# A two-layer hybrid decoder step on one core: where split operands are made and in which order they are queued

## The reference, cut

```python
x = LN(ALPHA * x + 0.5 * (silu(x @ w_gate) * (x @ w_up)) @ w_down)      # first feed-forward, width 2816
h = x @ w_in                      # pooling input | q | k | v | cross q | three gates of 1024
y_pool = causal pooling, four windows;  y_swa = sliding-window attention;  y_x = attention into 256 memory rows
merged = sum(sigmoid(gate_b) * (y_b @ w_br_b) for b in 3 branches)
x = LN(ALPHA * x + merged @ w_o)
x = LN(ALPHA * x + 0.5 * (silu(x @ w_gate) * (x @ w_up)) @ w_down)      # second feed-forward
```

## Time and profile before

| what | value |
|---|---|
| runs of the kernel before | 2546.69, 2549.53, 2554.24 us; median 2549.53 |
| profiled execution, device time | 2552.91 us |
| its span of instructions | 2551.1 us |
| granted clock of TensorE, mean | 0.982 |
| busy: PE, PEld, DVE, ACT, POOL | 2442.1, 2374.3, 1631.7, 1221.1, 615.6 us |
| instructions | 45264 |
| DMA | 220.63 MB, mean 86 GB/s |

### The profile page before, as it was taken

How to read it: one execution, slowest core, us unless ns; L and a number is a source line. 1 busy time by engine, 2 the same in 40 slices (tenths; PEclk the granted TensorE clock), 3 DMA queues, 4 the chain that set the end, 5 groups by cost and what they waited for, 6 DMA issues and landing times.

```text
span 2551.1 us, 45264 instructions
## 1 busy us (share of the span) xinstructions
PE 2442.1 (96%) x17684; PEld 2374.3 (93%) x17684; DVE 1631.7 (64%) x2716; ACT 1221.1 (48%) x2459; POOL 615.6 (24%) x544
## 2 busy tenths in 40 slices
PE   6999999999999999999999999989999999999997
PEld 6999999899999889999989999979999998999996
DVE  2878776435444587777687777664443447878775
ACT  4555555334422365655465556542342225655653
POOL 1333333120000123333323333321100002333332
PEclk9999999989999999999999999989999999999999
DMA  6132223222122212232213222222112222222221
GB/s 222 63 120 83 100 88 122 67 75 56 51 82 75 83 67 100 75 106 86 100 50 110 91 100 88 105 90 94 43 55 75 75 75 83 71 96 100 81 103 54
DMA packets 53523, 220.63 MB, mean 86 GB/s; under 512 B 15520, under 2 KB 18464, under 8 KB 40224
## 3 DMA queue, kind: packets, MB, share of 16 engines
q1 hardware_dynamic: 53312, 217.74, 25.1%
...
## 4 chain that ended last, share of the span: by engine, by line
PE 78%; DVE 12%; ACT 5%; DVEq 2%; issue 2%; DMA 0%; POOL 0%; ACTq 0%
PE pair L1796 12%; PE pair L1798 11%; PE pair L1797 11%; PE pair L1648 9%; PE pair L1650 9%; PE pair L1652 9%; PE S L1734 2%; DVE htl L1104 2%; PE S L1796 2%; PE S L1798 2%; PE S L1797 2%; ACT hth L660 1%; PE S L1890 1%; DVE TP L1024 1%; PE TP L1950 1%
## 5 line engine op out<-in xcount | busy, mean ns | idle before, releaser
L1796 PE MATMUL pair<-xth,hiA 128*128 128x288 f32 x1216 | 358.9, 295 | 13.9 <-ACT c L712 7.8
L1797 PE MATMUL pair<-xtl,hiA 128*128 128x288 f32 x1216 | 358.8, 295 | 0.0
L1798 PE MATMUL pair<-xth,loA 128*128 128x288 f32 x1216 | 358.4, 295 | 0.0
L612 ACT ACTIVATE hiA<-TP 128x512 fp32r<-128x512 f32 (+1 forms) x372 | 194.0, 555 | 220.0 <-DVE TP L1029 136.0
L1562 POOL TENSOR_TENSOR loB<-rawB,hiB 128x512 fp32r<-128x512 f32 (+1 forms) x128 | 159.5, 1247 | 480.2 <-ACT hiB L612 480.2
L1010 DVE TENSOR_TENSOR loA<-rawA,hiA 128x1024 fp32r<-128x1024 f32 x108 | 133.9, 1240 | 218.7 <-ACT hiA L599 218.3
L1648 PE MATMUL pair<-xh,hiA 128*128 128x288 f32 x1088 | 253.8, 310 | 18.9 <-DVE loA L1010 9.0
L1015 DVE TENSOR_TENSOR loA<-TP,hiA 128x512 fp32r<-128x512 f32 (+1 forms) x372 | 236.3, 635 | 31.7 <-ACT hiA L612 29.0
L1650 PE MATMUL pair<-xl,hiA 128*128 128x288 f32 x1088 | 243.0, 300 | 0.0
L1652 PE MATMUL pair<-xh,loA 128*128 128x288 f32 x1088 | 242.7, 300 | 0.0
L1796 PEld LDWEIGHTS pair<-xth,hiA 128*128 128x128 f32 x1216 | 228.0, 187 | 15.4 <-issue 15.3
...
## 6 DMA issues: line engine op xcount, KB each, us to landing
...
mcs<-in_mks SPq DMA_DIRECT2D x2, 2048.0 KB, 10.0
```

What stands on the lines that cost most here:

```text
L612: nc.scalar.activation(slot((hiA, hiB), prod, n), src, ACT.Copy).then_inc(f_hi, 1)
L1796: nc.tensor.matmul(bank, wt_hi, xt[0], start=start, stop=False, skip_group_check=True)
L1797: nc.tensor.matmul(bank, wt_hi, xt[1], start=False, stop=False, skip_group_check=True)
L1798: last = nc.tensor.matmul(bank, wt_lo, xt[0], start=False, stop=i == n - 1, skip_group_check=True)
```

## The change

Nothing is computed otherwise; the same products and sums are made. Blocks of the change:

1. Memory stage: the value pairs (pairs 1 and 3) get a split place of their own (`mwh`, `mwl`), so that ACT may round a pair while PE reads the one before; the copies of `x` move on ACT to behind pair 0, and on DVE to behind pair 2; the first fills of the feed-forward move to behind pair 2.
2. Feed-forward, head and first unit (u = 3): other places on ACT and DVE for the fills of unit 3, for the rounding of pair 0 and pair 1 of the hidden values, and for the copy `u2`.
3. Hidden pairs 3, 6 and 9: their first two forms are rounded in the iteration behind the four D units, the rest after the odd unit.
4. `norm_plain`: `tail_onto_x(3, 1)` and the split of block 1 stand after column tile 5 rather than after tile 7.
5. Merging: one list of 20 steps in place of ten steps twice; the packing of the weights, the counts and the gate slots follow it. The loops over it are otherwise the same.

```diff
-MERGE_STEPS = [(3, 0), (0, 4), (1, 4), (3, 1), (2, 4), (0, 5), (3, 4), (1, 5), (2, 5), (3, 5)]
-MERGED = (0, 1, 4, 5, 2, 3, 6, 7)
+MERGE_STEPS = [(3, 0), (0, 4), (1, 4), (3, 1), (2, 4), (0, 5), (3, 4), (1, 5), (2, 5), (3, 2)]
+MERGE_STEPS += [(0, 6), (3, 5), (1, 6), (3, 3), (2, 6), (0, 7), (3, 6), (1, 7), (2, 7), (3, 7)]
+MERGED = tuple(m for what, m in MERGE_STEPS if what == 3)
...
-H_GROUPS[3] = H_GROUPS[6] = [(0, 7)]
-H_GROUPS[9], H_GROUPS[10] = [(0, 4)], [(0, 2), (2, 3), (3, 4)]
+H_GROUPS[9], H_GROUPS[10] = [(0, 2), (2, 4)], [(0, 2), (2, 3), (3, 4)]
+PARTED = (6, 12, 18)
...
+        mwh = at("mwh", o_scr, [2, 1024], F32R)
+        mwl = at("mwl", o_ht + 32768, [2, 1024], F32R)
...
+        def split_of(qq):
+
+            return (mwh, mwl) if qq < PAIR_MEM and qq % 2 else (wh, wl)
...
 
-            def round_w(qq, s, first=False):
+            def round_w(qq, s):
 
                 act.wait_ge(raw_in[s], (qq + 1) * 16)
-                if not first:
+                if qq > 1 and qq <= PAIR_MEM:
+                    act.wait_ge(blk_done, qq * 2 + s - 3)
+                elif qq > PAIR_MEM:
                     act.wait_ge(blk_done, qq * 2 + s - 1)
-                nc.scalar.activation(wh[:, s, :], raw[:, s, :], ACT.Copy).then_inc(w_hi, 1)
+                nc.scalar.activation(split_of(qq)[0][:, s, :], raw[:, s, :], ACT.Copy).then_inc(w_hi, 1)
 
             def fill(fb, u, prod):
...
-                round_w(0, s, first=True)
-
-            for l in range(L):
-                for what in range(2):
-                    for s in range(2):
-                        act.wait_ge(blk_done, l * 4 + s + 1 if what == 0 else l * 4 + 4)
-                        n = (2 * what + s) * N_MEM
-                        nc.scalar.activation(mtmp[:, l, n:n + N_MEM], pair[s][:, 0, 0:N_MEM], ACT.Copy).then_inc(pair_free[s], 1)
-                        if l * 2 + what + 1 < PAIR_MEM:
-                            round_w(l * 2 + what + 1, s)
-                    if (l, what) == (1, 0):
-                        act.wait_ge(x_in, 16)
-                        for h in range(2):
-                            for c in range(KC):
-                                nc.scalar.activation(x_form((xth, xbh), h, c), x[:, c, half(h)], ACT.Copy).then_inc(xf_hi, 1)
-                        for q_no in range(4):
-                            fill_head(0, 0, q_no)
+                round_w(0, s)
+
+            for s in range(2):
+                round_w(1, s)
+            for i in range(PAIR_MEM):
+                for s in range(2):
+                    act.wait_ge(blk_done, 2 * i + s + 1 if i % 2 == 0 else 2 * i + 2)
+                    n = (2 * (i % 2) + s) * N_MEM
+                    nc.scalar.activation(mtmp[:, i // 2, n:n + N_MEM], pair[s][:, 0, 0:N_MEM], ACT.Copy).then_inc(pair_free[s], 1)
+                    if i + 2 < PAIR_MEM:
+                        round_w(i + 2, s)
+                if i == 0:
+                    act.wait_ge(x_in, 16)
+                    for h in range(2):
+                        for c in range(KC):
+                            nc.scalar.activation(x_form((xth, xbh), h, c), x[:, c, half(h)], ACT.Copy).then_inc(xf_hi, 1)
+                if i == 2:
+                    for q_no in range(4):
+                        fill_head(0, 0, q_no)
             for q_no in range(4):
                 fill_head(0, 1, q_no)
...
                 silu(1, 1)
-                round_sums(fb, 3)
-                round_hidden(fb, 0, 0)
-                round_hidden(fb, 0, 1)
-                silu(2, 0)
                 fill_a21(fb, HEADS)
                 fill(fb, HEADS, "P1")
+                round_sums(fb, 3)
                 fill(fb, HEADS, "P5")
+                round_hidden(fb, 0, 0)
+                silu(2, 0)
+                round_hidden(fb, 0, 1)
                 silu(2, 1)
                 fill(fb, HEADS, "P2")
                 fill(fb, HEADS, "P6")
...
                     if on:
                         copy_p1(fb, u)
                     if u == HEADS:
-                        round_hidden(fb, 1, 0)
+                        copy_u2()
                     elif on:
...
-                    if g:
-                        act.wait_ge(f_done, done(fb, u, "P6"))
-                        if u > HEADS:
-                            act.wait_ge(de_free, unit_count(fb, u - 1))
-                        nc.scalar.activation(u2[:, :], al[u % 2], ACT.Copy).then_inc(al_act, 1)
+                    if u == HEADS:
+                        round_hidden(fb, 1, 0)
+                    elif g:
+                        copy_u2()
...
-                    elif old and (j_old % 2 or len(groups) > 1):
+                    elif old and (j_old % 2 or j_old not in PARTED):
                         round_hidden(fb, j_old // 2, len(groups) - 1 if j_old % 2 else 0)
+                    elif not old and u > HEADS and SEQ[u - 1][2] == 3:
+
+                        act.wait_ge(f_done, done(fb, u - 1, "P3"))
+                        round_hidden(fb, SEQ[u - 2 - SEQ[u - 1][2]][1] // 2, 0)
...
                     rest_w(i, s)
-            for h in range(2):
-                for c in range(KC):
-                    dve.wait_ge(xf_hi, x_count(0, h, c))
-                    nc.vector.tensor_tensor(x_form((xtl, xbl), h, c), x[:, c, half(h)],
-                                            x_form((xth, xbh), h, c).bitcast(F32), ALU.subtract).then_inc(xf_lo, 1)
+                if i == 2:
+                    for h in range(2):
+                        for c in range(KC):
+                            dve.wait_ge(xf_hi, x_count(0, h, c))
+                            nc.vector.tensor_tensor(x_form((xtl, xbl), h, c), x[:, c, half(h)],
+                                                    x_form((xth, xbh), h, c).bitcast(F32), ALU.subtract).then_inc(xf_lo, 1)
 
             def add_residual(l, m, s):
 
...
                 rest_of_sums(fb, 1)
                 sums_of_x(fb, 3)
                 rest_of_sums(fb, 2)
+                first_sums(fb, HEADS)
                 head_hidden(fb, 1, 1)
                 hidden_sums(fb, 0)
                 hidden_sums(fb, 1)
                 rest_of_sums(fb, 3)
+                rest_of_sum(fb, HEADS, "P5")
+                second_sum(fb, HEADS)
                 rest_of_hidden(fb, 0, 0)
-                rest_of_hidden(fb, 0, 1)
-                first_sums(fb, HEADS)
                 dve.drain()
                 head_hidden(fb, 2, 0)
-                rest_of_sum(fb, HEADS, "P5")
-                second_sum(fb, HEADS)
+                rest_of_hidden(fb, 0, 1)
                 head_hidden(fb, 2, 1)
                 rest_of_sum(fb, HEADS, "P6")
                 third_sum(fb, HEADS)
                 rest_of_sum(fb, HEADS, "P7")
                 hidden_sums(fb, 2)
-                rest_of_hidden(fb, 1, 0)
 
             def ffn(fb):
 
...
                         hidden_sums(fb, j_old)
-                        if j_old % 2 or len(groups) > 1:
+                        if j_old % 2 or j_old not in PARTED:
                             rest_of_hidden(fb, j_old // 2, len(groups) - 1 if j_old % 2 else 0)
+                    elif u == HEADS:
+                        rest_of_hidden(fb, 1, 0)
+                    elif d_old and SEQ[u - 1][2] == 3:
+                        rest_of_hidden(fb, SEQ[u - 2 - SEQ[u - 1][2]][1] // 2, 0)
                     if more:
...
                     if c == 3:
                         rest_w(pq(l, Q_IN), 0)
                         tail_onto_x(fb, 2, 1)
+                    if c == 5:
+                        tail_onto_x(fb, 3, 1)
+                        rest_w(pq(l, Q_IN), 1)
                 rest_of_x(0, KC - 1)
-                tail_onto_x(fb, 3, 1)
-                rest_w(pq(l, Q_IN), 1)
                 tail_into_mean(2, 1)
                 tail_into_mean(3, 1)
                 center(l, 0, 1)
```

157 lines of the change are left out of this document (76 added, 81 removed).

## The result

| kernel | median of runs | lowest to highest | ratio to before (95%) |
|---|---|---|---|
| before | 2550.57 us (6 runs) | 2546.69 to 2554.24 | |
| changed | 2537.21 us (6 runs) | 2535.73 to 2540.39 | 0.9948 (0.9936 to 0.9961) |

The change makes the kernel 13.4 us faster, 0.5%. The prediction said 24.4 us and 2525 us, with a range of 2515 to 2537, and the median lies 0.2 us above that range. So the sign is right and the size is not: eleven microseconds are missing.

What follows compares the result with a forecast made beforehand. TensorE, busy 96% of the span, was taken as the bound, leaving its idle and half-clock time to win. 4.6 - 1.2 + 9.0 + 2.0 + 10.0 = 24.4 us off the 2549.5 median gave 2525 us, range 2515 to 2537.

Steps and rivals of the forecast that it cites:

- A: Memory stage: it ends at 45.25 in place of 49.85, a gain of 4.6 us, bounds 3 and 6.
- The walk: Memory stage, step by step: pair 1 starts at 24.4, pair 2 at 32.2, pair 3 at 38.6, end at 45.25.
- B: Feed-forward head and unit 3: a loss of 1.2 us in all, bounds a gain of 13.9 and a loss of 5.
- (1): Unit 3: P7's wait of 1.51 us goes, but u3 comes later and P4 waits; 0.25 us remain.
- (2): Unit 3: P5 needs the last head_hidden, which ends 0.2 us earlier; P5 would gain 0.45 us.
- (3): Unit 3: GpSimd's subtraction for P1 moves onto sums_of_x(3); one hit delays DVE's chain and P5 by 1.0 us.
- C: Joints behind down units: five forms instead of seven shorten the chain before c22; gain 9.0 us, bounds 7 to 10.
- D: norm_plain, twice: the split of block 1 ends earlier; gain 2.0 us, bounds 0 and 4.
- E: Merging, twice: the wait for S and the half clock behind it go; gain 10.0 us, bounds 8 and 10.5.
- B pays: Rival, head and unit 3: the four stalls were real, giving 2 to 14 us instead of -1.2; chance 0.12.
- the joint turns on the kernel: Rival, joints: DVE waiting for ACT in iteration 11 passes its 1.47 us cover, making the kernel slower; chance 0.04.
- one of 2 to 3 us before P5 instead of P1: Sign named for unit 3: in three feed-forwards a wait of this length moves from P1 to P5.

Runs made afterwards that it cites:

- kernel 7: Changed kernel with the DMA of x issued behind pair 2's and the copies of x taken up later, in two halves: 2540.47 us.
- kernel 8: Changed kernel with both copies out of PSUM ahead of the next two roundings on ACT, and the copies of x in two halves: 2534.43 us.
- kernel 4: Changed kernel with only unit 3's half of the new order undone (copy u2, round_hidden (1, 0)); the head's new order stays: 2536.90 us.
- kernel 9: Changed kernel with the fills of P6 and P2 of unit 3 swapped on ACT, nothing else: 2529.43 us.
- kernel 1: Changed kernel with head and unit 3 on ACT and DVE back in the order of before, all else kept: 2527.57 us.
- kernel 10: Changed kernel with another order of head and unit 3: last head_hidden and silus earlier, rest_of_hidden and round_hidden (1, 0) later: 2516.11 us.
- kernel 2: Kernel before with only the new order of head and unit 3 added: 2563.09 us, ratio 1.0042.
- kernels 3: Changed kernel with the last head_hidden ahead of rest_of_hidden (0, 1) on DVE and its silu ahead of round_hidden (0, 1) on ACT: 2526.06 us.

## Why the prediction was wrong, point by point

**A, the memory stage: right.** 4.0 us where 4.6 were forecast. The walk held step by step: 24.38 for 24.4, 32.50 for 32.2, 39.05 for 38.6, 45.83 for 45.25. Its two reasons were tested apart and both stand: x in front of pair 2 (kernel 7), and the copy behind a rounding (kernel 8). On the first, the Trainium skill ("DMA: Bandwidth & Descriptors", under "Queues, rings and completion order") says that a ring's descriptors are consumed in order; the runs agree, with 6.2 us to landing behind x and 3.7 without it.

**B, head and unit 3: this step failed.** Forecast -1.2 us, with 5 as the largest loss; measured -10.9 (B undone) and -11.2 (B alone), and -8.4 between the two traces. Its parts:
- (1), P4 in place of P7, was right: 1.27 us in place of 1.51. But kernel 4 shows that behind P5's wait the 1.51 would have gone by itself in three of the four feed-forwards.
- (2), the last `head_hidden` 0.2 us earlier, was right for DVE's list. The sum of x in front of both meetings starts at 912.28 before and at 901.86 in the changed kernel, 10.42 us earlier, and the last `head_hidden` ends 8.59 us earlier; of the 1.83 us between, the two meetings with GpSimd make 2.06. But its gain of 0.45 for P5 was put on all four feed-forwards and exists only where P1 had waited. In the first P1 waited for nothing, so P5's new wait of 1.52 us is a plain loss.
- (3) counted one meeting with GpSimd, 1.0 us. The first came as forecast (0.94 us, 909.61). But P2's fill moves forward with P1's, and its subtraction met `rest_of_hidden(0, 0)`: 1.1 us more, taken away by kernel 9. The prediction followed one of the two quarters that its own change of order moves.
- The largest part was in no step: the clock after the waits. P1's waits of 2.50 to 2.83 us had left it at 1.00 in the profile of before, and the prediction took that for granted; in kernel 1, with the same order, it fell behind two of three. In the changed kernel the waits of 2.96 to 3.19 us brought 6.4 us of loss.

In waits B costs 17.6 - 15.6 = 2.0 us, near the forecast, and that is in part luck: with the second meeting away (kernel 9) the waits are 13.1, so the order with one meeting, as forecast, gains 2.5 us of waits in place of losing 1.2, and the unseen meeting takes 4.5. With the clock B costs 8.4 in these traces, outside its bounds. The term was mis-sized because a wait was priced at its length alone at a place where, in stage A, the same text had priced the half clock behind one. "B pays", the first rival, was wrong for this order; in the order of kernel 10 the waits before P1 and P7 are gone and no long one takes their place, and it is 11.8 us faster than B undone, within the rival's 2 to 14.

**C, the joints: right.** P3 of units 12 and 22 starts 0.31 us late in all eight places, where it was 1.39 (once 1.75): 9.0 us, the number forecast. No wait appeared at units 11, 21 or 31, so "the joint turns on the kernel" didn't happen.

**D: right**, 2.1 us between the two traces where 2.0 were forecast, with luck in the size: the eleven traces with D scatter by almost 4 us, about a mean of some 3.

**E, merging: right.** 5.0 us in the first layer and 4.9 in the second by the starts of the products behind it, clock 1.00, no wait until the list's end, where 0.7 us stay.

Sum over the two traces: 4.0 - 8.4 + 9.0 + 2.1 + 9.9 = 16.6, where these two executions lie 17.2 us apart. Of the rest, 1.7 us lie behind the kernel's last wait, where nothing was changed (clock 0.84 before, 1.00 after), and the other places lose 1.1. The medians lie 13.4 apart; where the 3.8 us between traces and medians lie, no trace shows. That B costs 10.9 and 11.2 by the medians and 8.4 by this trace fits a clock that falls further in other executions, as in kernel 2's (0.72 behind all three waits, stretch 11.4 us longer), but was only argued. The test that the prediction named for B ("one of 2 to 3 us before P5 instead of P1") was seen, and the loss behind it was seven to nine times the term that was written beside it.

What stays open: what besides a wait's length decides whether the clock falls. In kernels 3 and 9 four of P5's waits were of 1.85 or 1.86 us, and the clock fell behind one of them.
